# A gather of one slot for 128 tokens, products in four 64x64 tiles, and six kept weight blocks

## The chip, the cores and the metric

The kernel runs on one core of a Trainium2 chip. The metric is the time of one execution on the device in microseconds (us). Before the change it is 1643.7 us, the median of 3 runs (1643.1 to 1644.28 us).

## The reference

Two layers over 256 tokens of width 1024. Each layer mixes tokens (two kinds of attention), then replaces the feed-forward part by an expert retrieval, and closes with a gated addition and a LayerNorm. The change is about the retrieval and what follows it:

```python
for i in range(DEPTH):                                   # 2 layers
    mix = token_mixers(h, w_in[i], w_out[i], ...)        # differential attention + sparse attention
    h = layer_norm(DEEPNORM_ALPHA * h + mix, ln1_g[i], ln1_b[i])
    r = DEEPNORM_ALPHA * h + peer_ffn(h, ...)
    gate = sigmoid(r @ ple_wg[i] + ple_bg[i])
    h = layer_norm(r + gate * (p[i] @ ple_wp[i]), ln2_g[i], ln2_b[i])

def peer_ffn(...):                                       # per token: 8 heads x 16 experts of 16384
    q = xt @ w_q;  s = q . sub_keys                      # 2 x 128 scores a head, top 16 of each half
    best, pos = top_k(all 256 sums, 16); g = softmax(best)
    u, v = u_tab[eidx], v_tab[eidx]                      # 128 rows of u and of v for each token
    return sum_k g_k * gelu(u_k . x) * v_k
```

Each token needs 128 rows of `u` and `v`. They lie side by side in one table (8 KB a pair), so 256 tokens x 128 slots x 2 layers x 8 KB = 537 MB are read.

## The kernel before, in words

The work is four runs (layer x tile of 128 tokens). Run n has a mixing stage (`MIX[n]`: projections, attention, output projection, LayerNorm, choice of the experts) and a closing stage (`CLOSE[n]`: gate, addition, LayerNorm). Four gather phases, one for each run, lie end to end. While phase n fetches and uses the expert rows of run n, the closing of run n-1 and the mixing of run n+1 are done beside it.

A phase has 64 pairs of gathers (`PAIRS`). One gather (L535, issued by GpSimd) brings 128 rows of 8 KB into one of 8 buffers of the ring `rows`. For each pair VectorE takes two dot products with the tokens (L1070) and, every second pair, spreads the softmax weights over small diagonal matrices `idg` (L1062). ScalarE takes the GELU (L707) and scales the diagonals to `dg` (L711). TensorE multiplies `dg` by the v half of the buffer and adds it to the accumulator `acc` in PSUM (L1390, in the last phase L1386). When that is done, GpSimd may refill the two buffers (`pair_done`).

A gather before the change holds four slots of 32 tokens: partition 32a+t is slot 4q+a of token 32c+t. So the index table must be rearranged by small products (`perm`, L1283, copied to `rows_of` and `g_of` in L944 and L945), and the tokens must be spread too: `hx[c]` holds the 32 tokens of block c four times (products L1361, copied by ScalarE through `spread_out`). The product's stationary matrix is 128x32, so a gather's two products fill the 32 partitions of block c.

The order on each engine is written out by hand: the tables (`PROJECT_PLAN`, `ATTEND_PLAN`, `TURN_PLAN`, `CLOSE_PLAN`, `LAST_EARLY`, `LAST_CLOSE`) give a part's pair on PE, ACT and DVE, and `walk` issues the parts of a pair ahead of the pair's own work. The start, before the first pair, is `START_PE`, `START_ACT`, `START_DVE`. Every engine works its list in order.

Weights come in blocks of 1 MB (two units), issued by SyncE in the order in which TensorE uses them (L493), into a ring of four buffers (`WRING`). `KEPT_BLOCKS` (four) have buffers of their own and are loaded once per layer instead of once per run. `EXTRA` (four) are blocks of the first run that land in ring buffers 4 to 7 of `rows` before the gathers need them.

The last phase works in blocks of 32 tokens (order 0, 2, 1, 3): each block is closed as soon as its products are done. Its parts are `ztake` (ScalarE copies it out of `acc`), `zrT` (transposes), `zgate` (bias and gate products L1324, L1332, sigmoid), `zblend` (VectorE L966 to L970), `zsum` (L1340) and `znorm` (L975 to L987). `warm` (L1346) are products whose result nobody reads.

## Time and profile before

| | |
|---|---|
| median of 3 runs | 1643.7 us (1643.1 to 1644.28) |
| profiled execution, its own time | 1645.81 us |
| its span, first to last instruction | 1644.0 us |
| PE, DVE, ACT, POOL busy | 75%, 65%, 29%, 36% of the span |
| moved by the DMA engines | 662.10 MB, 403 GB/s on average |
| mean granted TensorE clock | 0.836 |

PE is TensorE, DVE VectorE, ACT ScalarE, POOL GpSimd, SP SyncE. The busy shares are averages over the whole span. Which resource sets the pace has to be read stretch by stretch. DMA shares can read 1.01 or 1.02 where all 16 DMA engines are busy throughout. A matrix product in 32-bit floats stands as two MATMUL records in the profile.

### The profile page before, as it was taken

How to read it: one execution, taken by the hardware profiler on the slowest of the kernel's cores; microseconds unless marked ns; L12 is line 12 of the kernel's file. 1: busy time of each engine (PE TensorE's matmuls, PEld its weight loads, DVE VectorE, ACT ScalarE, POOL GpSimd, SP SyncE). 2: the span in 40 equal slices, each digit the busy share in tenths (PEclk: the TensorE clock that was granted, in tenths of full speed). 3: DMA queues.
4: the chain of work that ended last, by engine and by line, in shares of the span. 5: the costliest groups of instructions: out<-in, count | busy, mean ns of one | idle time of the engine just before them, and what ended most of it. 6: DMA issues, size and time to landing. Idle time of an engine off the chain costs nothing.

```text
span 1644.0 us, 19823 instructions
## 1 busy us (share of the span) xinstructions
PE 1227.3 (75%) x7210; PEld 620.1 (38%) x7210; DVE 1070.7 (65%) x2773; ACT 479.5 (29%) x1278; POOL 585.3 (36%) x516
## 2 busy tenths in 40 slices
PE   8988958696778789586677969869687767434556
PEld 8655714241452266131442328424253223111223
DVE  1458788755689764654579785584588958655553
ACT  1323224342223423241132422342222323211223
POOL 0013243343334333343334332244344434444441
PEclk9999978897899889897888979979798876555558
DMA  8789999999999999999999999999999999999994
GB/s 315 255 328 412 418 420 410 422 422 421 421 409 406 406 422 420 422 420 422 420 421 421 418 410 412 421 421 422 421 419 417 414 421 414 422 421 421 419 419 166
DMA packets 92625, 662.10 MB, mean 403 GB/s; under 512 B 10288, under 2 KB 11504, under 8 KB 12528
## 3 DMA queue, kind: packets, MB, share of 16 engines
q0 software_dynamic: 73728, 536.90, 78.9%
q1 hardware_dynamic: 18576, 123.81, 18.6%
q8 instruction: 57, 0.93, 0.2%
q14 instruction: 40, 0.33, 0.0%
q10 hardware_dynamic: 224, 0.13, 0.0%
HBM read 659.75 MB, written 1.05 MB: 402 GB/s over the span
## 4 chain that ended last, share of the span: by engine, by line
DMA 38%; PE 30%; DVE 21%; ACT 5%; issue 3%; POOL 3%; ACTq 0%; SPq 0%; DVEq 0%; POOLq 0%
DMA rows<-uv_dram,rows_of 37%; DVE rows L1070 10%; PE bank L1110 9%; PE acc L1390 8%; PE bank L1128 5%; POOL rows L535 3%; PE acc L1386 2%; ACT dg L711 2%; PE bank L1332 1%; ACT ex L630 1%; PE bank L1353 1%; ACT gel L707 1%; DVE i L778 1%; DVE i L769 1%; DVE ex L772 1%
## 5 line engine op out<-in xcount | busy, mean ns | idle before, releaser
L535 POOL DMA_INDIRECT rows<-uv_dram,rows_of x512 | 585.1, 1143 | 1025.4 <-PE acc L1390 663.0
L1070 DVE CUSTOM_DVE_ANT_0 rows<-rows,hx 128x1024 f32<-128x1024 f32 x512 | 618.7, 1224 | 425.8 <-DMA rows<-uv_dram,rows_of 412.7
L1390 PE MATMUL acc<-rows,dg 128*32 128x512 f32 x1536 | 439.7, 707 | 234.6 <-ACT dg L711 232.9
L707 ACT ACTIVATE gel<-dots 128x2 f32<-128x2 f32 x256 | 52.0, 203 | 853.2 <-DVE dots L1070 841.4
L1390 PEld LDWEIGHTS acc<-rows,dg 128*32 128x32 f32 x1536 | 83.5, 119 | 497.5 <-ACT dg L711 323.4
L1110 PEld LDWEIGHTS bank<-xT,wring 128*128 128x128 f32 x1728 | 206.1, 200 | 32.2 <-issue 25.2
L1386 PE MATMUL acc<-rows,dg 128*32 128x256 f32 x1024 | 109.9, 571 | 144.6 <-ACT dg L711 144.6
L1110 PE MATMUL bank<-xT,wring 128*128 128x128 f32 x1728 | 213.0, 285 | 4.4 <-ACT xT L550 2.4
L1128 PE MATMUL bank<-wring,xT 128*128 128x512 f32 x352 | 165.5, 617 | 0.8 <-ACT xT L550 0.7
L711 ACT ACTIVATE dg<-idg,gel 128x32 f32<-128x32 f32 x512 | 137.1, 314 | 23.8
L1386 PEld LDWEIGHTS acc<-rows,dg 128*32 128x32 f32 x1024 | 35.4, 145 | 213.0 <-ACT dg L711 183.8
L1128 PEld LDWEIGHTS bank<-wring,xT 128*128 128x128 f32 x352 | 66.6, 197 | 91.3 <-issue 89.3
L707 ACT ACT_TABLE_LOAD x52 | 66.7, 1283 | 1.2
L1110 PEld LDWEIGHTS bank<-xT,kept 128*128 128x128 f32 x384 | 45.6, 198 | 5.6 <-issue 5.4
L1110 PE MATMUL bank<-xT,kept 128*128 128x128 f32 x384 | 47.6, 284 | 0.0
L550 ACT ACTIVATE probsT<-bank 128x512 f32<-128x512 f32 (+1 forms) x59 | 31.2, 545 | 53.9 <-PE bank L1110 27.2
L1070 DVE DVE_READ_ACCUMULATOR2_ANT dots<- 128x1 f32 x512 | 42.2, 82 | 0.0
L1237 PE MATMUL bank<-prm,fixed 64*128 64x256 f32 x96 | 31.0, 476 | 11.0 <-DVE mixed L957 11.0
L1062 DVE TENSOR_TENSOR idg<-fixed,g_of 128x128 f32<-128x128 f32 x128 | 36.9, 288 | 2.0 <-ACT dg L711 0.5
L1361 PE MATMUL bank<-h,fixed 128*128 128x512 f32 x64 | 31.4, 616 | 0.0
L1237 PEld LDWEIGHTS bank<-prm,fixed 64*128 64x128 f32 x96 | 21.3, 233 | 21.2 <-DVE mixed L957 12.0
L818 DVE SCALAR_TENSOR_TENSOR sc<-fixed,bank 128x128 f32<-128x128 f32 (+1 forms) x32 | 9.1, 349 | 26.7 <-PE bank L1188 26.7
(185 smaller groups left out, 1057.4 us busy)
## 6 DMA issues: line engine op xcount, KB each, us to landing
wring<-wmix_dram SPq DMA_DIRECT2D x84, 1024.0 KB
wring<-wclose_dram SPq DMA_DIRECT2D x15, 1024.0 KB
kept<-wmix_dram SPq DMA_DIRECT2D x8, 1024.0 KB, 18.4
rows<-uv_dram,rows_of POOLq DMA_INDIRECT x512
rows<-wmix_dram SPq DMA_DIRECT2D x4, 1024.0 KB, 12.7
rows<-prm_dram SPq DMA_DIRECT2D x2, 1024.0 KB, 7.9
wring<-wmix_dram SPq DMA_DIRECT2D x4, 512.0 KB
fixed<-fixed_dram SPq DMA_DIRECT2D x1, 576.0 KB, 10.6
```

Source lines behind the costliest of these rows:

```text
L535: pool.indirect_dma_start(out=rows[:, slot, :], out_offset=None, in_=uv_d[phase // TILES], in_offset=bass.IndirectOffsetOnAxis(ap=rows_of[ ...
L550: ins = A(out, src, func)
L707: A(gel[:, s:s + 2], dots[:, s:s + 2], ACT.Gelu).then_inc(gelu_done, 1)
L711: A(dg[:, s + j, :], idg[:, P // 2 % 2, 2 * (P % 2) + j, :], ACT.Identity, scale=gel[:, s + j:s + j + 1]).then_inc(dg_ready, 1)
L1062: V.tensor_tensor(idg[:, P // 2 % 2], ident32[:, None, :].broadcast_to([128, 4, BT]), gates[:, :, None].broadcast_to([128, 4, BT]), ALU.mu ...
L1070: V.tensor_tensor_reduce(out=rows[:, s, 0:D], in0=rows[:, s, 0:D], in1=hx[:, c, :], scale=1.0, scalar=0.0, op0=ALU.mult, op1=ALU.add, accu ...
L1110: ins = MM(bk[:, T * at:T * at + T], w[:, T * c:T * c + T], src[:, c, :], start=(c == 0), stop=(c == KC - 1))
L1128: ins = MM(bk[:], xT[:, 2 * q + c, :], w[:, 512 * c:512 * c + 512], start=(q == 0 and c == 0 and extra is None), stop=(q == 3 and c == 1), ...
L1237: ins = MM(bk[:, QCOLS * j:QCOLS * j + QCOLS], chooser(first + i // 2, 2 * (i % 2) + j), prm[:], start=True, stop=True)
L1361: MM(bk[:], fixed[:, F_SPREAD + 128 * c:F_SPREAD + 128 * c + 128], h[:, 512 * i:512 * i + 512], start=True, stop=True).then_inc(full, 1)
L1386: ins = MM(quarters(acc, c)[BT * k:BT * k + BT, :], dg[:, s, :], rows[:, s, D + 256 * k:D + 256 * k + 256], start=False, stop=False, skip_ ...
L1390: ins = MM(acc[BT * c:BT * c + BT, 512 * i:512 * i + 512], dg[:, s, :], rows[:, s, D + 512 * i:D + 512 * i + 512], start=False, stop=False ...
```

## The change

It has five parts.

1. In the first three phases a gather brings one slot of all 128 tokens (`columns_of`). Its indices are a column of the index table as VectorE computes it, so the `perm` products and copies go in those phases, and the dots read the tokens themselves (`hb`, one buffer for each tile) instead of `hx`. The last phase keeps the old form.
2. The product of a gather in those phases is four products of 64x64 tiles: row half r of the gather, column half j of the output. `dg` is 128x64. The accumulator then holds token half r in PSUM bank r and feature half j in partition half j. So the closing reads `rT` in another order, and new products `nat` bring the rows back to their natural layout.
3. `hx` for the last phase lies in two kept weight blocks, and its spreading matrices in a third, loaded when that block is done. The freed memory makes six kept blocks. Two blocks instead of four are extra.
4. At a turn of phases ScalarE only copies the accumulator (`take`). `mixed` shares the memory of `res`, and the gates that of the queries.
5. In the last phase the third block's closing is laid out anew: gate at pair 59, blend at pair 62 instead of 61, its norm behind the last pair. `warm` is issued twice instead of four times, and the bias products (`zbias`) are a part of their own.

```diff
-def gathers_of(phase, p):
-
-    if phase < RUNS - 1 or p < PAIRS // 2:
-        return [(p // 2, 2 * (p % 2)), (p // 2, 2 * (p % 2) + 1)]
+TILE_ORDER = ((0, 0), (1, 1), (0, 1), (1, 0))
...
+    if phase < LAST or p < PAIRS // 2:
+        return [2 * p, 2 * p + 1]
...
 ]
-TURN_PLAN = [
-    ("hx0", 61, None, None), ("hx1", 62, None, None), ("hx2", 63, None, None),
-    ("hx3", 64, None, None), ("hx", None, 64, None), ("init", 64, None, None),
+TURN_PLAN = [("take", None, 64, None), ("init", 64, None, None)]
+TURN_LAST = [
+    ("hx0", 60, 61, None), ("hx1", 61, 62, None), ("hx2", 62, 63, None),
+    ("hx3", 63, 64, None), ("take", None, 64, None), ("init", 64, None, None),
...
+    ("g1a", 4, None, None), ("g1b", 5, 6, None), ("nat", 6, None, None), ("gb0", 6, 7, None), ("gb1", 7, 8, None),
...
-def last_close(c, at, step=1):
-
-    return [(f"ztake{c}", None, at + 1 * step, None), (f"zrT{c}", at + 2 * step, at + 3 * step, None),
-            (f"zgate{c}", at + 4 * step, at + 5 * step, None), (f"zblend{c}", None, None, at + 5 * step),
-            (f"zsum{c}", at + 6 * step, None, None), (f"znorm{c}", None, at + 7 * step, at + 7 * step)]
-
-
-LAST_EARLY = [("zple", 5, 6, None), ("zgb", 26, 27, None), ("warm0", 60, None, None), ("warm1", 61, None, None),
-              ("warm2", 62, None, None), ("warm3", 63, None, None)]
-for _i in range(BLOCKS - 1):
+def last_close(c, at):
+
+    return [(f"ztake{c}", None, at + 1, None), (f"zrT{c}", at + 2, at + 3, None),
+            (f"zbias{c}", at + 4, None, None), (f"zgate{c}", at + 4, at + 5, None), (f"zblend{c}", None, None, at + 5),
+            (f"zsum{c}", at + 6, None, None), (f"znorm{c}", None, at + 7, at + 7)]
+
+
+LAST_EARLY = [("zple", 5, 6, None), ("zgb", 26, 27, None), ("warm0", 61, None, None)]
+for _i in range(BLOCKS - 2):
     LAST_EARLY += last_close(LAST_ORDER[_i], PAIRS // 2 + PAIRS // 2 // BLOCKS * (_i + 1))
-LAST_CLOSE = last_close(LAST_ORDER[BLOCKS - 1], 0, 0)
+_c, _d = LAST_ORDER[BLOCKS - 2:]
+LAST_EARLY += [(f"ztake{_c}", None, 57, None), (f"zrT{_c}", 58, 59, None), (f"zbias{_c}", 59, None, None), (f"zgate{_c}", 59, 61, None),
+               (f"zblend{_c}", None, None, 62), (f"zsum{_c}", 62, None, None), ("warm1", 62, None, None)]
+LAST_CLOSE = [(f"ztake{_d}", None, 0, None), (f"zbias{_d}", 0, None, None), (f"zrT{_d}", 0, 0, None), (f"znorm{_c}", None, 0, 0),
+              (f"zgate{_d}", 0, 0, None), (f"zblend{_d}", None, None, 0), (f"zsum{_d}", 0, None, None), (f"znorm{_d}", None, 0, 0)]
...
 START_PE = ("wake T par idx dq0 dq1 dk0 dk1 iw ds0 ix sq0 sq1 dv0 dv1 dpt sk0 dpv sk1 ss0 sv0 sv1 mT0 mix0a spt0 spt1 mix1p spv mix1a mT1 "
-            "mix0b mix1b fill h1T pq0a ps0 pq1a init hx0 ps1 hx1 perm0 pq2a hx2 hx3").split()
+            "mix0b mix1b fill h1T pq0a ps0 pq1a init ps1 pq2a").split()
 START_ACT = ("embed0 T par idx dq1 dk1 iw ix exps0 exps1 sq1 dv1 dpt dpv sk1 rms sexp0 sexp1 sv1 mT0 spt0 spt1 mT1 embed1 n1a "
-             "h1T pq0a ps0 C0a pq1a hx0 ps1 hx1 hx2 hx3").split()
-START_DVE = ("embed0 ds0 ix sel0 sel1 wts0 wts1 sel2 sel3 far rms rms2 ss0 merge embed1 n1a n1b A0a B0a C0a C0b perm0").split()
+             "h1T pq0a ps0 C0a pq1a ps1").split()
+START_DVE = ("embed0 ds0 ix sel0 sel1 wts0 wts1 sel2 sel3 far rms rms2 ss0 merge embed1 n1a n1b A0a B0a C0a C0b").split()
...
+            if part[:4] == "perm" and run.n < LAST:
+                continue
...
-EXTRA_SLOT = 4
-EXTRA = [tuple(units_of(part)) for part in ("pq1a", "pq2a", "pq2b", "pq3a")]
+EXTRA_SLOT = 6
+EXTRA = [tuple(units_of(part)) for part in ("pq1a", "pq2a")]
 
 KEPT = WRING + len(EXTRA)
-KEPT_BLOCKS = [(U_SK, U_SK + 1)] + [tuple(units_of(part)) for part in ("pq3b", "pq4a", "pq4b")]
+KEPT_BLOCKS = [tuple(units_of(part)) for part in ("pq2b", "pq3a", "pq3b")] + [(U_SK, U_SK + 1)] + [
+    tuple(units_of(part)) for part in ("pq4a", "pq4b")]
+HX_BLOCKS, SPREAD_BLOCK = 2, 2
...
-        hx = sb("hx", [128, BLOCKS, D])
+        hx = kept[:, 0:HX_BLOCKS, :].rearrange("p b (a d) -> p (b a) d", d=D)
+        spread = kept[:, SPREAD_BLOCK, 0:128 * BLOCKS]
-        h, res, mixed = (sb(n, [128, D]) for n in ("h", "res", "mixed"))
+        hb, res = sb("hb", [128, TILES, D]), sb("res", [128, D])
+        mixed = res
...
+                if part == "hx0":
+                    sp.wait_ge(*block_done[KEPT + SPREAD_BLOCK, run.layer])
+                    sp.dma_start(spread, fixed_d[:, FCOLS:FCOLS + 128 * BLOCKS]).then_inc(spread_landed, 16)
...
-                        if EXTRA_SLOT <= k < RING:
+                        if EXTRA_SLOT <= k < EXTRA_SLOT + len(EXTRA):
                             pool.wait_ge(*block_done[WRING + k - EXTRA_SLOT, 0])
                         pool.indirect_dma_start(
                             out=rows[:, slot, :], out_offset=None, in_=uv_d[phase // TILES],
...
-                            in_offset=bass.IndirectOffsetOnAxis(ap=rows_of[:, phase % 2, 4 * q + c:4 * q + c + 1], axis=0),
+                            in_offset=bass.IndirectOffsetOnAxis(ap=rows_of[:, phase % 2, col:col + 1], axis=0),
...
-                    for i in range(2):
-                        take(run, f"rT{i}", quarter(xT, i))
+                    for r in range(2):
+                        act.wait_ge(*full_at(run, f"rT{r}"))
+                        bk, taken = bank_of(run, f"rT{r}")
+                        A(xT[:, :, HT * r:HT * r + HT].rearrange("p (j k) t -> p j k t", j=2),
+                          bk[:].rearrange("p (k j t) -> p j k t", k=4, j=2), ACT.Copy).then_inc(taken, 1)
...
-                if part == "hx":
-                    if n:
-                        act.wait_ge(dot_ready, 4 * QUADS * n)
-                    for c in range(BLOCKS):
-                        if n and c == 2:
-                            taking(CLOSE[n - 1])
-                        spread_out(run, c)
+                if part == "take":
+                    taking(CLOSE[n - 1])
...
-                    A(dg[:, s + j, :], idg[:, P // 2 % 2, 2 * (P % 2) + j, :], ACT.Identity, scale=gel[:, s + j:s + j + 1]
+                    w = HT if phase < LAST else BT
+                    A(dg[:, s + j, 0:w], idg[:, P // 2 % 2, 2 * (P % 2) + j, 0:w], ACT.Identity, scale=gel[:, s + j:s + j + 1]
...
+                    bk, taken = bank_of(run, f"nat{i}")
+                    for name in banks_of(run, "nat"):
+                        dve.wait_ge(*full_at(run, name))
+                    V.tensor_tensor(half_of(res, i), bk[:], half_of(gates, i), ALU.add).then_inc(taken, 1)
+                    dve.wait_ge(*taken_at(run, f"nat{i}"))
...
-                        dve.wait_ge(out_stored, 16)
...
+                    if n < LAST:
+                        V.scalar_tensor_tensor(rows_of[:, n % 2, at], sel[:, 0, 0:gs], float(NKEYS), sel[:, 1, 0:gs], ALU.mult, ALU.add
+                                               ).then_inc(rows_picked, 1)
...
+                    w, one = (HT, ident64) if phase < LAST else (BT, ident32)
+                    V.tensor_tensor(idg[:, P // 2 % 2, :, 0:w], one[:, None, :].broadcast_to([128, 4, w]),
+                                    shares[:, :, None].broadcast_to([128, 4, w]), ALU.mult).then_inc(idg_ready, 1)
...
+                    if phase < LAST:
+                        if col == 0:
+                            dve.wait_ge(h1_ready, 2 * phase + 2)
+                        tokens = hb[:, phase % TILES, :]
+                    else:
+                        if col < BLOCKS:
+                            dve.wait_ge(hx_ready, col + 1)
+                        tokens = hx[:, col % BLOCKS, :]
...
+                if part == "nat":
+                    for j in range(2):
+                        bk, full = bank(run, f"nat{j}")
+                        at = slice(HT * j, HT * j + HT)
+                        for r in range(2):
+                            ins = MM(bk[HT * r:HT * r + HT, :], ident[at, at], res[at, 512 * r:512 * r + 512], start=True, stop=True,
+                                     skip_group_check=True)
+                        ins.then_inc(full, 1)
...
+                    pe.wait_ge(h1_ready, 2 * n + 2)
+                    for r, j in TILE_ORDER:
+                        at = slice(HT * r, HT * r + HT)
+                        MM(acc[HT * j:HT * j + HT, 512 * r:512 * r + 512], ident_a[at, at], h_of(run)[at, 512 * j:512 * j + 512],
+                           start=True, stop=False, skip_group_check=True)
...
-                        ins = MM(acc[BT * c:BT * c + BT, 512 * i:512 * i + 512], dg[:, s, :],
-                                 rows[:, s, D + 512 * i:D + 512 * i + 512], start=False, stop=False, skip_group_check=True)
+                    for r, j in TILE_ORDER:
+                        at = slice(HT * r, HT * r + HT)
+                        ins = MM(acc[HT * j:HT * j + HT, 512 * r:512 * r + 512], dg[at, s, :], rows[at, s, D + 512 * j:D + 512 * j + 512],
+                                 start=False, stop=False, skip_group_check=True)
```

On SyncE's queue these are the weight loads of the second run's mixing and what follows, before and after the change (`wring` is the weight ring, `wmix` the mixing weights, `wclose` the closing weights). Before:

```order
L493 DMA wring<-wmix_dram 128x2048 x9
L493 DMA kept<-wmix_dram 128x2048
L493 DMA rows<-wmix_dram 128x2048 x4
L493 DMA kept<-wmix_dram 128x2048 x3
L493 DMA wring<-wmix_dram 128x2048
L493 DMA wring<-wmix_dram 128x1024
L493 DMA wring<-wmix_dram 128x2048 x21
L493 DMA wring<-wclose_dram 128x2048
```

After:

```order
L515 DMA wring<-wmix_dram 128x2048 x9
L515 DMA kept<-wmix_dram 128x2048
L515 DMA rows<-wmix_dram 128x2048 x2
L515 DMA kept<-wmix_dram 128x2048 x5
L515 DMA wring<-wmix_dram 128x2048
L515 DMA wring<-wmix_dram 128x1024
L515 DMA wring<-wmix_dram 128x2048 x19
L515 DMA wring<-wclose_dram 128x2048
```

The first run's two blocks moved from `rows` to `kept`, and the second run issues 19 whole blocks instead of 21. The fourth run's list changes in the same way.

On PE at the start, from the transposes of h to the first pair's product (L1100 or L1138 are transposes, L1110 or L1148 query products, L1273 or L1311 key products, L1374 or L1424 the accumulator's start). Before:

```order
L1100 MATMUL bank<-fixed,h 128x128 x8
L1110 MATMUL bank<-xT,wring 128x128 x16
L1273 MATMUL bank<-kept,probsT 128x128 x2
L1110 MATMUL bank<-xT,rows 128x128 x16
L1374 MATMUL acc<-h,fixed 128x512 x2
L1361 MATMUL bank<-h,fixed 128x512 x2
L1273 MATMUL bank<-kept,probsT 128x128 x2
L1361 MATMUL bank<-h,fixed 128x512 x2
L1283 MATMUL bank<-chosen,fixed 32x8 x16
L1110 MATMUL bank<-xT,rows 128x128 x16
L1361 MATMUL bank<-h,fixed 128x512 x4
L1110 MATMUL bank<-xT,rows 128x128 x16
```

After:

```order
L1138 MATMUL bank<-fixed,hb 128x128 x8
L1148 MATMUL bank<-xT,wring 128x128 x16
L1311 MATMUL bank<-kept,probsT 128x128 x2
L1148 MATMUL bank<-xT,rows 128x128 x16
L1424 MATMUL acc<-hb,fixed 64x512 x4
L1311 MATMUL bank<-kept,probsT 128x128 x2
L1148 MATMUL bank<-xT,rows 128x128 x16
L1148 MATMUL bank<-xT,kept 128x128 x16
L1442 MATMUL acc<-rows,dg 64x512 x8
```

The spreading products and the index products are gone, and the accumulator's start is four 64-wide products.

On DVE at the end, the third block's blend and norm (L966 to L970 and L975 to L987; after the change L987 to L991 and L996 to L1007) among the dots of the last pairs. Before:

```order
L970 BN_STATS stats<-res 128x6
L1070 ISA rows,dots<-rows,hx 128x1024
L1070 ISA dots 128x1
L1070 ISA rows,dots<-rows,hx 128x1024
L1070 ISA dots 128x1
L1062 TENSOR_TENSOR idg<-fixed,g_of 128x128
L1070 ISA rows,dots<-rows,hx 128x1024
L1070 ISA dots 128x1
L1070 ISA rows,dots<-rows,hx 128x1024
L1070 ISA dots 128x1
L975 BN_AGGR mv<-bank 128x2
```

After:

```order
L991 BN_STATS stats<-res 128x6
L1094 TENSOR_TENSOR idg<-fixed,g_of 128x4x32
L1108 ISA rows,dots<-rows,kept 128x1024
L1108 ISA dots 128x1
L1108 ISA rows,dots<-rows,kept 128x1024
L1108 ISA dots 128x1
L1108 ISA rows,dots<-rows,kept 128x1024
L1108 ISA dots 128x1
L1108 ISA rows,dots<-rows,kept 128x1024
L1108 ISA dots 128x1
L996 BN_AGGR mv<-bank 128x2
```

Before, the blend lies ahead of the dots of pair 61 and the norm ahead of those of the last pair, 63. After, the blend lies ahead of pair 62 and the norm behind all dots.

## Rows read from the trace of the kernel before

**Rows 1.** The page: DMA engines' busy tenths in 40 slices, and GB/s.

```profile
DMA  8789999999999999999999999999999999999994
GB/s 315 255 328 412 418 420 410 422 422 421 421 409 406 406 422 420 422 420 422 420 421 421 418 410 412 421 421 422 421 419 417 414 421 414 422 421 421 419 419 166
```

**Rows 2.** Busy time of each engine in stretches, with granted clock, DMA share and GB/s.

```profile
core 0: us, PE busy (x) PEld busy (x) DVE busy (x) ACT busy (x) POOL busy (x), PEclk, DMA share, GB/s
111.00:119.00 8.00, 6.88 (x64) 4.25 (x63) 6.88 (x30) 3.04 (x7) 1.31 (x2) 1.00 0.02 7
135.00:488.00 353.00, 275.67 (x1604) 146.10 (x1605) 254.46 (x694) 103.95 (x284) 130.72 (x118) 0.87 1.01 418
488.00:524.00 36.00, 27.63 (x128) 9.34 (x129) 34.62 (x107) 14.08 (x34) 15.55 (x14) 1.00 0.97 389
524.00:960.00 436.00, 337.11 (x1688) 157.73 (x1685) 284.63 (x732) 130.72 (x344) 161.23 (x140) 0.89 1.01 419
960.00:1000.00 40.00, 30.52 (x147) 15.03 (x146) 37.95 (x107) 12.61 (x34) 17.71 (x14) 0.79 0.99 399
1618.00:1623.00 5.00, 2.75 (x20) 1.01 (x19) 4.42 (x9) 1.20 (x6) 0.00 (x0) 0.87 0.13 54
```

**Rows 3.** Waits: engine line <- released by: us in total, times, longest.

```profile
POOL rows L535 <- PE acc L1390: 663.0, 181, 10.6
DVE rows L1070 <- DMA rows<-uv_dram,rows_of: 412.7, 257, 3.8
```

**Rows 4.** Timeline, PE's products in a middle stretch: start us, us, instructions.

```profile
628.13 1.71 PE L1188 MATMUL bank<-dkT,dqT 64*128 64x128 f32 x16
629.77 1.92 PE L1390 MATMUL acc<-rows,dg 128*32 128x512 f32 x8
631.62 0.72 PE L1196 MATMUL bank<-ikT,iqT 64*128 64x128 f32 x8
```

**Rows 5.** Groups of instructions by form: busy us, mean ns, idle before.

```profile
L1361 PE MATMUL bank<-h,fixed 128*128 128x512 f32 x64 | 31.4, 616 | 0.0
L1062 DVE TENSOR_TENSOR idg<-fixed,g_of 128x128 f32<-128x128 f32 x128 | 36.9, 288 | 2.0 <-ACT dg L711 0.5
L1022 DVE TENSOR_TENSOR ex<-posf,fixed 128x256 f32<-128x256 f32 x16 | 6.8, 422 | 0.3
```

**Rows 6.** Timeline, start: from the chosen indices to the first gather's issue.

```profile
115.70 0.17 DVE L1043 SCALAR_TENSOR_TENSOR chosen<-sel 128x16 f32<-128x16 f32 x1
116.93 0.18 DVE L944 CAST rows_of<-bank 128x16 uint32<-128x16 f32 x1 [0.57 <-PE bank L1283]
117.39 1.07 POOL L535 DMA_INDIRECT rows<-uv_dram,rows_of  x1 [116.94 <-DVE rows_of L944]
```

**Rows 7.** Timeline, the third block's closing and the last pairs.

```profile
1608.87 1.23 DVE L1070 CUSTOM_DVE_ANT_0 rows<-rows,hx 128x1024 f32<-128x1024 f32 x1 [1.25 <-DMA rows<-uv_dram,rows_of]
1616.30 0.43 DVE L966 TENSOR_TENSOR mixed<-mixed,val 128x256 f32<-128x256 f32 x1 [6.20 <-ACT mixed L550]
1621.89 3.59 PE L1346 MATMUL bank<-fixed 128*128 128x512 f32 x4
1626.30 0.27 DVE L975 BATCH_NORM_AGGREGATE mv<-bank 128x2 f32<-128x24 f32 x1 [3.89 <-PE bank L1340]
1628.92 1.22 DVE L1070 CUSTOM_DVE_ANT_0 rows<-rows,hx 128x1024 f32<-128x1024 f32 x1
1631.07 0.59 PEld L1386 LDWEIGHTS acc<-rows,dg 128*32 128x32 f32 x16 [2.71 <-ACT dg L711]
1631.07 1.07 PE L1386 MATMUL acc<-rows,dg 128*32 128x256 f32 x16 [1.89 <-ACT dg L711]
```

**Rows 8.** Timeline: one block's gate products twice, and the same pair product.

```profile
1567.91 4.93 PE L1332 MATMUL bank<-wring,xT 128*32 128x256 f32 x64
1586.41 1.94 PE L1386 MATMUL acc<-rows,dg 128*32 128x256 f32 x16 [2.94 <-ACT dg L711]
1633.57 3.66 PE L1332 MATMUL bank<-wring,xT 128*32 128x256 f32 x64
```

159 lines of the change are left out of this document (82 added, 77 removed), and 3 rows, old and new, of tables (CLOSE_LAST, CLOSE_PLAN).

## The prediction

> **What bounds the kernel now.** I read the DMA lines of the page first. From the fourth of 40 slices to the last but one the DMA engines are 90% busy or more and move 406 to 422 GB/s. Only the first 120 us and the last slice are lower [rows 1]. The table of stretches says the same more sharply: DMA share 1.01 and 418 to 419 GB/s in the long stretches, while PE is busy for 275.7 of 353 us (78%) [rows 2]. So for nine tenths of the span the bytes set the time. Then the waits: GpSimd waits 663 us for PE's products to free ring buffers, and VectorE 412.7 us for rows to land [rows 3]. That is a full ring behind a saturated DMA, not a slow PE. What is left for the rest is what happens before the first gather, two shallow dips at turns of phases, and the tail behind the last rows.
>
> **Part 1, six kept blocks: 9.9 us.** Runs 2 and 4 each issue two whole weight blocks fewer, which the queue's rows in the section on the change show. The first run loads the same blocks into other buffers. Four blocks of 1.049 MB at 419 GB/s [rows 2] are 4 x 2.50 = 10.0 us. The spreading matrices and the shorter constants add 32 KB net, 0.1 us. Both phases in which the loads fall are saturated, so the 9.9 us come off the span if PE can walk 1.3% faster there. It has 22% idle time. Bounds: 0 (something else paces these phases at once) and 10.
>
> **Part 2, the start: 1.2 us.** The index column is ready in 115.70, 0.17 us long. Before the change it went through PE and was copied only at 116.93, and the gather was issued at 117.39, 0.28 us after that copy's end [rows 6]. Now the instruction of 115.70 writes `rows_of` itself: 115.70 + 0.17 + 0.28 = 116.15, 1.24 us earlier. The DMA engines stand still meanwhile (share 0.02 from 111 to 119 [rows 2]), so this counts in full. The eight spreading products of the start go too (31.4 us for 32 such products, 0.98 each [rows 5], 7.9 us on PE), but VectorE's choice is what the gather waits for, so I give nothing for it. Bounds: 0 and 1.5.
>
> **Part 3, the turns: 1 us.** Before, the first dots of a phase had to wait until ScalarE had copied all of `hx`, which could only start behind the old phase's last dots. Now they need only h and their rows. At the two turns with a dip the DMA share is 0.97 for 36 us and 0.99 for 40 us, against 1.01 [rows 2]: 1.4 + 0.8 = 2.2 us lost. The accumulator must still be copied and restarted ahead of the first product, so I take 1.0. Bounds: 0 and 2.2.
>
> **Part 4, the products of 64x64 tiles: nothing.** Today a pair is 4 products, 8 records, 1.92 us at full clock [rows 4]. Only two column blocks are in it, so two records run at a time: four steps of 0.43 us and 0.2 us around them. Each new product fills a quarter of the array as the old one did, but a pair has 8 of them, 16 records. Four at a time gives four steps again, 1.92 us. Two at a time gives 8 x 0.43 + 0.2 = 3.6 us, one at a time 7.1 us. The trace has four column tiles at once: the last phase's pair is 16 records of half the width in 1.07 us, 0.2 us around four steps of 0.216 us [rows 7]. It has two row tiles at once: 8 records of L1196 take 0.72 us, where 16 of L1188, issued in longer groups for each row half, take 1.71, 0.107 each, one after the other [rows 4]. Rows and columns together it does not have. I take 1.92 us, because both nearest rows overlap fully when the tiles alternate as closely as they do here. Up to 3.3 us (below) it costs nothing either way.
>
> A rule of the Trainium skill speaks against this. Its page "TensorE: Matmul & The Clock Gate", section "The mechanism", says that a weight load overlaps products in flight only if its row group is another. Two of our four tiles share a row group with their forerunners. By that rule some loads would be exposed and a pair would be nearer to the 3.6 us. The trace disagrees: the four column tiles of [rows 7] share one row group, and their 16 loads lie within the first 0.59 us of the 1.07. The page "TensorEngine Tiling (Array Packing)", "Gotcha 1", says that different row tiles must not write one PSUM bank at the same time. The new form gives row half r bank r, so the rule costs nothing here, and no row of before shows its price.
>
> **Part 5, VectorE and ScalarE: nothing.** `idg` doubles to 256 columns: 0.29 us becomes 0.42 (a 256-column operation of the same kind) [rows 5], 0.13 x 96 = 13 us over three phases, and the index copies and 24 of 32 `hx` halves' copies go. VectorE is busy for 254 of 353 us and the dots wait for rows [rows 2, 3], which hides it. The new `nat` products (four a closing, three closings) are 12 of at most 0.98 us on PE, whose idle time hides them. If that cover is gone they cost up to 12 us.
>
> **Part 6, the end: 4 us.** Most engines have delivered the last rows by 1618, stragglers until 1623 (share 0.13 [rows 2]). But VectorE is in order and stands idle for 6.2 us until the third block's gate is through ScalarE at 1616.30, and for 3.9 us until its sums are there at 1626.30. The sums were behind idle products (L1346, 3.59 us at 1621.89). So the last dot starts only at 1628.92, and its product at 1631.07 [rows 7]. After the change the gate is one pair earlier, the blend one pair later, and nothing lies before the last dots. The last dot can start when its row is there, about 1623.0. From there on the chain is the old one, so it ends 5.9 us earlier. The norm of the third block slips under the last block's gate products. Something is late next: the clock. The last gate ran at 2.4 GHz in 3.66 us, behind four sets of idle products. Two sets are gone. The same 64 records took 4.93 us where they began at 1.2 GHz and got 2.4 on the way, and the pair product takes 1.94 us at 1.2 GHz instead of 1.07 [rows 8]. That gives back 0 (clock kept) to 4.5 us (all at 1.2 GHz: 3.7 + 0.9). I take 1.9. The end gains 4.0 us, bounds 1.4 and 5.9.
>
> **Sum.** 9.9 + 1.2 + 1.0 + 0 + 0 + 4.0 = 16.1 us. The profiled execution took 1645.8 us, 1.8 us of it outside its span of 1644.0. That makes 1629.7 us. The median of the runs is 2.1 us below the profiled execution, so the forecast is 1627.6 us. With each term at its likely bounds (loads 9 to 10, start 1 to 1.5, turns 0 to 2.2, end 1.4 to 5.9) the gain is 11.4 to 19.6, 1624.1 to 1632.3 us.
>
> **Rivals.**
>
> *A, the tiles run two at a time (slower).* A pair's product is 3.6 us, 1.7 us more. From 135 to 1000 us PE is busy for 671 of 865 us and serves 143 pairs [rows 2], so it has 194 us idle, 1.36 us a pair. From 3.3 us a pair on PE is the bound. At 3.6 it needs 246 us more, 52 more than it has. If half of its idle time can't be used, since products wait for their rows, it is 149. Over 192 pairs that is 70 to 200 us: some 1700 to 1830 us, 1740 near its lower end. For it: no row has rows and columns tiled together. Against it: both halves of the pattern overlap. 5%.
>
> *B, a gather of 128 tokens' same slot moves fewer bytes per us (slower).* The indices of a gather are now the same rank of one head for all tokens, not four ranks of 32. If the rows of one gather fall worse on the memory, the rate drops. In slices 13 and 14 the same gathers ran at 406 GB/s instead of 421 [rows 1], 3.6%. Over 384 gathers of 2.5 us that is 34 us: 1627.6 + 34 = 1662 us. It decides from a rate below 414 on. Against it: every row is 8 KB wherever it lies, and the engines read at a full share throughout. 4%.
>
> *C, the end does not get shorter.* The stragglers of the last gather or the clock take it all: 1627.6 + 4 = 1632 us. 14%.
>
> *D, the loads saved are not given back,* because the pace of the second or fourth run's mixing is set by its own chain of parts: half of part 1 is lost, 1633, or all of it, 1637.5. For it: the parts are tied to pairs, and the waits on PE are long. Against it: the DMA share of 1.01. 10%.
>
> *E, more than I count* (deeper prefetch through kept blocks closes more of the dips, the start gains from a freer PE): 1622 us. 7%.
>
> *F, no effect at all*, because the freed buffers and the shorter queues only move waits: 1643. 4%.
>
> The forecast has the other 56%. Faster by over 0.2% (3.3 us, about what a measurement of this kernel can tell from no change) are the forecast, C, D and E: 87%. F is within it: 4%. A and B are slower: 9%. The range for 8 in 10 takes in E's and D's times: 1620 to 1638 us. It leaves out A, B, F and what lies beyond, some 15%.
>
> **What would show it.** The product's line must have 3072 records in three phases, 16 a pair in about 1.9 us at full clock. At 3.6 us A is right. The bytes must be about 658 MB with a rate of 418 GB/s or more in the long stretches; below 414 B is right. The first gather must be issued near 116.1 us. The stretch between the first gathers of the second and third phase holds no saved load and should shorten by 1 us at most, those of the first and third phase by 5 each. If they don't, D is right. At the end the last dot must wait for its row and for nothing else, and the last gate's 64 records show the clock: 3.7 us, or 5 and more. I am wrong if PE is busy over 95% in the long stretches, or if VectorE waits in the last pairs for anything but rows.

## The result, and the profile after

The changed kernel takes 1638.14 us (median of 13 runs, 1629.99 to 1641.75), the kernel before 1646.61 us beside it (13 runs, 1643.1 to 1653.32). The ratio is 0.9943 [0.9927, 0.9959]: 9.4 us faster. Forecast were 16.1 us and a time of 1627.6 us, with a range of 1620 to 1638.

The page of the changed kernel's profiled execution (its own time 1641.7 us):

```profile
span 1639.9 us, 21801 instructions
DMA  8689999999999999999999999999999999999994
GB/s 314 252 342 398 412 420 384 423 421 421 421 419 372 420 377 421 421 421 421 420 421 421 420 421 415 420 421 414 420 421 420 420 420 409 422 422 421 421 421 183
DMA packets 92201, 658.07 MB, mean 401 GB/s; under 512 B 10240, under 2 KB 11456, under 8 KB 12608
```

658.07 MB were moved instead of 662.10: the four saved blocks of 1.049 MB, less 0.16 MB of other transfers. Yet the mean rate fell. Against [rows 1] the slices from the 25th on are about as good. The new dips are the 4th, 7th, 13th and 15th slice: 398, 384, 372 and 377 GB/s.

The stretches of [rows 2], in the changed kernel:

```profile
core 0: us, PE busy (x) PEld busy (x) DVE busy (x) ACT busy (x) POOL busy (x), PEclk, DMA share, GB/s
135.00:488.00 353.00, 279.38 (x1892) 151.84 (x1884) 258.95 (x684) 107.14 (x284) 135.39 (x117) 0.87 1.00 413
488.00:524.00 36.00, 22.72 (x116) 6.58 (x120) 34.66 (x103) 10.79 (x27) 12.81 (x12) 0.76 0.94 366
524.00:960.00 436.00, 334.63 (x2060) 161.23 (x2052) 284.42 (x715) 130.58 (x335) 159.80 (x140) 0.87 1.01 416
960.00:1000.00 40.00, 28.57 (x182) 12.82 (x183) 37.99 (x105) 11.82 (x35) 15.03 (x13) 0.75 1.01 416
1618.00:1623.00 5.00, 1.34 (x17) 0.42 (x16) 2.96 (x8) 0.81 (x5) 0.00 (x0) 0.86 0.03 13
```

The first turn (488 to 524 us) fell from 389 to 366 GB/s, and TensorE's clock there from 1.00 to 0.76. VectorE is busy for 34.66 of the 36 us, as it was before. The second turn (960 to 1000 us) got better, 399 to 416 GB/s. The last bytes come some 2.5 us earlier.

The products of the new form, in the groups by line and in the timeline (start us, us). These rows answer to [rows 4], [rows 5] and [rows 6]:

```profile
L1442 PE MATMUL acc<-rows,dg 64*64 64x512 f32 x3072 | 463.4, 728 | 248.7 <-ACT dg L735 248.6
L1094 DVE TENSOR_TENSOR idg<-fixed,g_of 128x256 f32<-128x256 f32 (+1 forms) x128 | 49.8, 389 | 2.0
```

```profile
115.34 0.17 DVE L1065 SCALAR_TENSOR_TENSOR rows_of<-sel 128x16 uint32<-128x16 f32 x1
115.80 1.07 POOL L560 DMA_INDIRECT rows<-uv_dram,rows_of  x1 [115.34 <-DVE rows_of L1065]
...
501.70 3.69 PE L1442 MATMUL acc<-rows,dg 64*64 64x512 f32 x16 [1.74 <-ACT dg L735]
506.91 1.95 PE L1442 MATMUL acc<-rows,dg 64*64 64x512 f32 x16 [1.52 <-ACT dg L735]
...
628.21 1.95 PE L1442 MATMUL acc<-rows,dg 64*64 64x512 f32 x16
```

A pair of 16 records takes 1.95 us at 2.4 GHz and 3.69 us at 1.2 GHz. The second figure is no tiling effect: it nearly doubles with the clock.

The end, in the timeline, answering to [rows 7]:

```profile
1616.28 1.23 DVE L1108 CUSTOM_DVE_ANT_0 rows<-rows,kept 128x1024 f32<-128x1024 f32 x1 [1.13 <-DMA rows<-uv_dram,rows_of]
1621.20 1.23 DVE L1108 CUSTOM_DVE_ANT_0 rows<-rows,kept 128x1024 f32<-128x1024 f32 x1 [1.23 <-DMA rows<-uv_dram,rows_of]
...
1616.31 1.96 PE L1386 MATMUL bank<-fixed 128*128 128x512 f32 x4
1618.43 1.07 PE L1437 MATMUL acc<-rows,dg 128*32 128x256 f32 x16 [0.16 <-ACT dg L735]
1623.36 1.94 PE L1437 MATMUL acc<-rows,dg 128*32 128x256 f32 x16 [3.85 <-ACT dg L735]
1625.22 1.08 PE L1361 MATMUL bank<-prm,fixed 64*32 64x256 f32 x8
1626.23 0.69 PE L1356 MATMUL bank<-fixed,res 128*128 128x128 f32 x2
1627.39 5.81 PE L1372 MATMUL bank<-wring,xT 128*32 128x256 f32 x64 [0.47 <-ACT xT L575]
```

The last dots now wait for rows alone. But the clock is at 1.2 GHz from the last pair on: its product takes 1.94 us, and the last gate 5.81 us, against 1.07 and 3.66 in [rows 7, 8].

**An account of the span.** The span splits into three parts that can be read from the DMA records of any profile here: up to the first gather, from it to the last gathered byte, and from there to the end. The middle part is compared with what its bytes need at 422.8 GB/s (on each of 16 engines an 8 KB packet every 310 ns; in these traces 309 ns is the commonest and 312 ns the median time of such a packet). The rest of it is called the lost time: engines dry, or packets slower than that.

| profiled run | first gather | bytes need | lost time | last byte to end | span |
|---|---|---|---|---|---|
| before | 117.4 | 1481.4 | 24.5 | 20.8 | 1644.0 |
| changed | 115.8 | 1472.4 | 32.6 | 19.1 | 1639.9 |

So 9.0 us of bytes are gone, the end is 1.7 us shorter, the start 1.6 us, and 8.1 us came back as lost time. The experiments are read by the same account, because the start of one kernel differs by up to 7 us from execution to execution (110.6 to 117.4 us in the 18 profiles here, in both families), which would drown a term of 1 us. Each line of the account is one execution: the same kernel, profiled twice, lost 32.6 and 30.6 us.

The prediction also named the distances between the first gathers of the phases as a sign. They went from 378.4 to 379.0 us in the first phase, from 399.9 to 403.9 in the second and from 385.3 to 379.3 in the third. Only the third shortened as forecast.

### The profile page after: what moved, and what is told of

The parts are those of the page before. It is cut to its first block, busy times and chain, and to the rows that moved or that the text cites. A ratio compares the mean times of both kernels' runs of the same rounds, so it can differ in the third digit from the quotient of the medians.

```text
span 1639.9 us, 21801 instructions
## 1 busy us (share of the span) xinstructions
PE 1212.4 (74%) x8246; PEld 625.5 (38%) x8246; DVE 1081.0 (66%) x2743; ACT 477.5 (29%) x1257; POOL 589.1 (36%) x516
## 2 busy tenths in 40 slices
DMA packets 92201, 658.07 MB, mean 401 GB/s; under 512 B 10240, under 2 KB 11456, under 8 KB 12608
## 4 chain that ended last, share of the span: by engine, by line
DMA 37%; PE 32%; DVE 19%; ACT 5%; POOL 3%; issue 3%; ACTq 0%; SPq 0%; POOLq 0%; DVEq 0%
DMA rows<-uv_dram,rows_of 37%; PE bank L1148 9%; PE acc L1442 9%; DVE rows L1108 9%; PE bank L1166 6%; POOL rows L560 3%; PE acc L1437 2%; ACT dg L735 2%; PE bank L1372 1%; PE bank L1138 1%; PE bank L1401 1%; ACT ex L655 1%; DVE idg L1094 1%; ACT gel L730 1%; DVE i L802 1%
## 5 line engine op out<-in xcount | busy, mean ns | idle before, releaser
L1108 DVE CUSTOM_DVE_ANT_0 rows<-rows,hb 128x1024 f32<-128x1024 f32 x384 | 463.2, 1223 | 316.6 <-DMA rows<-uv_dram,rows_of 315.3
L1442 PE MATMUL acc<-rows,dg 64*64 64x512 f32 x3072 | 463.4, 728 | 248.7 <-ACT dg L735 248.6
L1442 PEld LDWEIGHTS acc<-rows,dg 64*64 64x64 f32 x3072 | 113.5, 154 | 512.9 <-ACT dg L735 346.2
L1108 DVE CUSTOM_DVE_ANT_0 rows<-rows,kept 128x1024 f32<-128x1024 f32 x128 | 155.5, 1224 | 113.9 <-DMA rows<-uv_dram,rows_of 113.5
L1148 PEld LDWEIGHTS bank<-xT,wring 128*128 128x128 f32 x1536 | 181.8, 199 | 25.9 <-issue 18.8
L1148 PE MATMUL bank<-xT,wring 128*128 128x128 f32 x1536 | 187.6, 284 | 4.7 <-DVE sc L842 2.9
L735 ACT ACTIVATE dg<-idg,gel 128x64 f32<-128x64 f32 (+1 forms) x512 | 147.0, 334 | 24.6 <-ACT gel L730 0.7
L1437 PEld LDWEIGHTS acc<-rows,dg 128*32 128x32 f32 x1024 | 35.3, 146 | 218.6 <-ACT dg L735 190.0
L1148 PEld LDWEIGHTS bank<-xT,kept 128*128 128x128 f32 x640 | 73.7, 193 | 14.1 <-issue 14.1
L1148 PE MATMUL bank<-xT,kept 128*128 128x128 f32 x640 | 77.0, 279 | 0.0
L1094 DVE TENSOR_TENSOR idg<-fixed,g_of 128x256 f32<-128x256 f32 (+1 forms) x128 | 49.8, 389 | 2.0
## 6 DMA issues: line engine op xcount, KB each, us to landing
wring<-wclose_dram SPq DMA_DIRECT2D x15, 1024.0 KB, 10.4
```

The source lines that it names most:

```text
L735: A(dg[:, s + j, 0:w], idg[:, P // 2 % 2, 2 * (P % 2) + j, 0:w], ACT.Identity, scale=gel[:, s + j:s + j + 1]).then_inc(dg_ready, 1)
L1094: V.tensor_tensor(idg[:, P // 2 % 2, :, 0:w], one[:, None, :].broadcast_to([128, 4, w]), shares[:, :, None].broadcast_to([128, 4, w]), ALU ...
L1108: V.tensor_tensor_reduce(out=rows[:, s, 0:D], in0=rows[:, s, 0:D], in1=tokens, scale=1.0, scalar=0.0, op0=ALU.mult, op1=ALU.add, accum_out ...
L1148: ins = MM(bk[:, T * at:T * at + T], w[:, T * c:T * c + T], src[:, c, :], start=(c == 0), stop=(c == KC - 1))
L1437: ins = MM(quarters(acc, c)[BT * k:BT * k + BT, :], dg[:, s, 0:BT], rows[:, s, D + 256 * k:D + 256 * k + 256], start=False, stop=False, sk ...
L1442: ins = MM(acc[HT * j:HT * j + HT, 512 * r:512 * r + 512], dg[at, s, :], rows[at, s, D + 512 * j:D + 512 * j + 512], start=False, stop=Fal ...
```

## The experiments

Each kernel was timed in five rounds beside the kernel before on the same chip. Four kernels at a time shared a chip: a_same, a_heat, a_warm3 and a_reload; a_oldend, b_newend, a_actidg and a_dbl; a_nat, c_warm3, c_heat and a_tiles; a_narrow, a_repair, b_dbl and b_actidg. Ratios are to the kernel before.

**a_same: the changed kernel itself.** It is the base of the others.

> The changed kernel itself once more, as the measure for the runs beside it. Theory (slow products at the turns): again 7 to 10 us below the kernel before, DMA engines dry for 3 to 4 us more than before in the stretches where VectorE is over 90% busy (140 to 180, 260 to 290, 490 to 600 us), and pair products of 3.5 us and more there where the granted clock is at its lower level. Rival (slower gathers as such): the rate is lower also in the long stretches where VectorE has time to spare.

1635.6 us, ratio 0.9931 [0.9913, 0.9948]. Account: first gather 110.8, lost 30.6, last byte to end 18.4, span 1632.1. So the gain is 9 to 11 us by the two measurements.

**a_reload: two of the six kept blocks are loaded again in the second and fourth run.**

```
-    return [b for b in blocks if not (run.stage == "mix" and run.tile and b in KEPT_BLOCKS)]
+    return [b for b in blocks if not (run.stage == "mix" and run.tile and b in KEPT_BLOCKS[HX_BLOCKS:])]
```

> The two blocks kept in addition are loaded again in the second and fourth run, as before the change: 4 x 1.049 MB more. Theory (bytes set the time): 8 to 10 us slower than the changed kernel, so about the time of the kernel before. Rival (the phases that lost loads are paced by their own chain, the saved loads are not given back): at most 5 us slower.

1645.97 us, ratio 0.999 [0.9978, 1.0002]: 10.4 us above a_same. Its weights' queue moved 4.2 MB more:

```profile
q1 hardware_dynamic: 18720, 123.84, 18.5%
```

With the bytes of before, and all else changed, the time of before is nearly back. Lost time is 31.5 us, as in the changed kernel. The saved loads give what they should. Everything else in the change together gives 1 to 2 us (by the interval between nothing and 3.6), where 6.2 were forecast. The distances between first gathers say the same of each phase: 383.3 and 384.2 us in the first and third, 377.1 and 378.5 in a_same.

**a_heat: idle products at the first two turns,** four sets of two in each, to hold the clock.

```
+TURN_PLAN = [("heat0", 61, None, None), ("heat1", 62, ...), ("heat2", 63, ...), ("heat3", 64, ...), ("take", ...
```

> Four sets of two 128x512 products that nobody reads stand where the spreading products of the first two turns stood. Theory (the removed products had kept the clock at 2.4 GHz over the turn, and slow pair products let the DMA engines run dry): granted clock about 1.0 from 490 to 530 us, first pair product of the second phase 1.95 instead of 3.6 us, DMA share there back to 0.98, and the kernel 1.5 to 4 us faster than the changed kernel. Rival (VectorE alone sets the pace at the turn): clock up, time the same within 1 us or up to 2 us slower, since the products stand in the way of the pairs.

1636.14 us, ratio 0.993 [0.9912, 0.9948], the same as a_same. The turn itself did change:

```profile
488.00:524.00 36.00, 30.13 (x151) 10.64 (x150) 34.69 (x103) 10.95 (x28) 15.21 (x13) 1.00 0.97 391
```

Clock 1.00 and 391 GB/s, as before the change. Lost time is 29.1 us, 1.5 less than in a_same, and the last byte to end is 19.9, 1.5 more. The time shows no gain, but the interval would let 4 us of either sign pass, and the idle products themselves stand in the way of the pairs. So this run does not price the clock at the turn.

**a_warm3: a third warm set at pair 63.**

```
+               ..., ("warm1", 62, None, None), ("warm2", 63, None, None)]
```

> One more set of idle products ahead of the last pair's product. Theory (the end lost 3 to 4 us to the lower clock): last pair product 1.1 instead of 1.9 us, last gate 3.7 instead of 5.8 us, 2 to 3.5 us faster than the changed kernel. Rival (the chain from the last landed row sets the end in any case): no more than 0.5 us, or slower if the set delays the last product.

1634.59 us, ratio 0.9915 [0.9901, 0.9929], about 1 us below a_same, which its interval does not separate. In the timeline of its end:

```profile
1621.88 1.07 PE L1437 MATMUL acc<-rows,dg 128*32 128x256 f32 x16 [1.94 <-ACT dg L735]
...
1624.37 3.66 PE L1372 MATMUL bank<-wring,xT 128*32 128x256 f32 x64 [0.47 <-ACT xT L575]
```

The clock holds, and the last byte to end is 15.4 us. Three other kernels (a_tiles, a_narrow, a_actidg) have 15.4 to 15.5 us without this set. So two sets hold the clock in some executions, in three of the ten profiles that have two. Three or four sets held it in all eight.

**a_oldend and b_newend: the order of the end alone,** taken back in the changed kernel, and put into the kernel before.

```
-LAST_EARLY += [(f"ztake{_c}", None, 57, None), (f"zrT{_c}", 58, 59, None), (f"zbias{_c}", 59, None, None), ...
-LAST_CLOSE = [(f"ztake{_d}", None, 0, None), (f"zbias{_d}", 0, None, None), (f"zrT{_d}", 0, 0, None), ...
+LAST_CLOSE = last_close(LAST_ORDER[BLOCKS - 1], 0, 0)        # a_oldend; b_newend the other way round
```

> The changed kernel with the order of the end as it was before: the third quarter's bias, gate and sum and the fourth's take come after the last pair again, the bias stands behind the transposes, four warm sets at pairs 60 to 63. What is computed is the same. If the end is worth what the forecast gave it (4.0 us), this run lies 4.0 us above the changed kernel (1635.6 us in the calls before), at 1639 to 1640. If the end is worth little, because TensorE stands at 1.2 GHz behind the last pair of the changed kernel (last gate 5.81 us there against 3.66 before, last dot to the end of the span 18.7 against 15.1 us) and one warm set more brought only 1 us, it lies 0 to 1.5 us above, at 1635.5 to 1637.

> The kernel before with the changed kernel's order of the end and nothing else of the change. Full value of the end: 4.0 us below the kernel before. Little value: 0 to 1.5 us below it. If it is 4 here and less than 1.5 in the changed kernel, the end is worth its price only where the last gathers land as in the kernel before.

a_oldend: 1638.7 us, ratio 0.9939 [0.9917, 0.9961]. b_newend: 1642.36 us, ratio 0.9977 [0.9961, 0.9992], so 3.8 us faster than before, between 1.3 and 6.4. a_oldend's interval allows no difference and 4 us. The last byte to end is 20.8 us in before and 18.2 in b_newend, 19.3 in a_oldend against 19.1 and 18.4 in the changed kernel. Over all profiles it is 20.3 to 20.8 us in the three with the old end in the kernel before, and 15.4 to 19.9, 18.1 on average, in the nine variants of the changed kernel with the new end and two warm sets. The end's new order is worth 0.4 to 5.4 us from execution to execution, and 2.4 on average. In a_oldend VectorE waits 3.88 us for sums ahead of the last pair's dots, as in [rows 7], but the clock is kept (last dot to end 15.0 us). In b_newend the wait is gone and the clock too:

```profile
1620.91 1.94 PE L1393 MATMUL acc<-rows,dg 128*32 128x256 f32 x16 [3.85 <-ACT dg L716]
...
1624.94 4.79 PE L1339 MATMUL bank<-wring,xT 128*32 128x256 f32 x64 [0.47 <-ACT xT L555]
```

With the third warm set both are had: 15.4 us, 5.4 less than before.

**a_actidg: the diagonals are built by ScalarE.**

```
-   V.tensor_tensor(idg[:, P // 2 % 2, :, 0:w], one[...], shares[...], ALU.mult).then_inc(idg_ready, 1)      # VectorE, every second pair
+   A(idg[:, P // 2 % 2, 2 * (P % 2) + j, 0:w], one, ACT.Identity, scale=g_of[:, phase % 2, col:col + 1])     # ScalarE, ahead of the pair's GELU
```

> The changed kernel with the gated diagonals (idg) built by ScalarE, two of 128x64 a pair, where VectorE built four at a time in 0.42 us every second pair; what is computed is the same. VectorE loses 0.21 us a pair, in all 96 x 0.42 + 32 x 0.29 = 50 us of busy time; ScalarE (27% busy) gains about 0.33 us per token column. Theory V: the DMA engines go dry at the turns and at 570 to 600 us because VectorE is over 90% busy there and a pair costs it 5.8 us where the gathers need 5.05; each of some 30 such pairs then gives back 0.21 us: 5 to 8 us, 1628 to 1631. Theory N: VectorE's load is not what makes the ring dry (the slow clock of TensorE or the order of the loads is): within 1.5 us of the changed kernel, or slower by what the fuller ScalarE costs.

1630.95 us, ratio 0.9905 [0.9886, 0.9924]: 4.3 us below a_same by the ratios, at the edge of the noise. The groups by line show where the work went:

```profile
L741 ACT ACTIVATE idg<-fixed,g_of 128x64 f32<-128x64 f32 (+1 forms) x512 | 143.5, 329 | 3.2 <-DVE g_of L1089 1.7
```

The new instructions take 143.5 us on ScalarE, and those that went had 49.8 on VectorE. On the pages ScalarE's busy time rises from 477.5 to 596.3 us and VectorE's falls from 1081.0 to 1041.6. Lost time falls to 26.2 us. Two more pairs of kernels below differ in the diagonals alone: by the ratios c_warm3 is 4.0 us below a_warm3, and c_heat 5.3 us below a_repair, with 25.8 against 31.6 and 25.0 against 31.3 us lost. Three times the same: this gain is shown.

**a_dbl: each diagonal is built twice by VectorE.**

```
+   V.tensor_tensor(idg[:, P // 2 % 2, :, 0:w], ...).then_inc(L.sem, L.one()); settle()      # and then the same again
```

> The changed kernel with each gated diagonal built twice in the same place by VectorE (0.42 us more every second pair, 0.29 in the last phase, and a wait for its own result). Theory V: the mirror of the run that takes it away, 5 to 8 us slower (1641 to 1644); by the same slope the widening from 0.29 to 0.42 us in the change itself cost some 1.5 to 2.5 us. Theory N: within 1.5 us of the changed kernel, and the widening cost nothing.

1639.07 us, ratio 0.9947 [0.9926, 0.9968]: 2.6 us above a_same, where 5 to 8 were expected. The intervals overlap, and the changed kernel's other measurement was 0.9943, so the time shows no difference. Lost time is 35.9 us, 5 more than in a_same and 3 more than in the first profile of the changed kernel.

**b_actidg and b_dbl: the same two edits in the kernel before,** where a diagonal is 32 wide (37 us less, 37 us more).

> The kernel before with the gated diagonals built by ScalarE: VectorE loses 37 us. Same sensitivity as in the changed kernel: 2 to 3.5 us faster than the kernel before (ratio 0.998 to 0.9985). If the kernel before had slack on VectorE, under 1 us either way, and the changed kernel is the one in which the load on VectorE counts.

> The kernel before with each gated diagonal built twice in its place: VectorE gets 128 x 0.29 = 37 us more, and a wait for its own result. If the kernel before is as sensitive as the changed one (0.05 to 0.09 us for each us of VectorE's load): 2 to 3.5 us slower than the kernel before. If it had slack: under 1 us.

b_actidg: 1645.16 us, ratio 0.9994 [0.9975, 1.0013], lost time 25.2 us. b_dbl: 1648.92 us, ratio 1.0007 [0.9992, 1.0023], lost time 28.9 us. The kernel before shows nothing to gain from a lighter VectorE (25.2 against 24.5 and, in b_newend, 26.3 us lost). With a heavier one its one profile lost some 4 us more, but its time did not move beyond its interval. That the kernel before stands at a knee over which the change pushed it is therefore not shown.

**a_narrow: diagonals 32 wide in the changed kernel,** with the other columns set to zero once at the start. Half of each product is left out of the result.

```
-                    w, one = (HT, ident64) if phase < LAST else (BT, ident32)
+                    w, one = BT, ident32
```

> The changed kernel with the gated diagonals written 32 wide, as before the change; the other 32 columns are zero, so half of each product is left out of the result, while products, their shapes and gathers are unchanged. Only VectorE's load falls, by 96 x 0.13 us = 12.5 us. If the time goes with VectorE's load along the whole way (50 us less gave 4.3 us of time, 49 us more cost 2.6): 0.6 to 1.1 us below the changed kernel (1635), and dry or slow time of the gather stretch 30. If the widening is what ate the missing time: 4 to 5 us below (1631), dry or slow time 25 to 26 us as before the change.

1634.18 us, ratio 0.9916 [0.99, 0.9933], lost time 30.0 us. The time is 1 to 2.5 us below a_same, which the intervals do not separate, and the lost time is that of the changed kernel. VectorE is busy for 1068.5 us on this page, where the kernel before has 1070.7 and loses 24.5. So more load on VectorE as a whole is not what loses the time.

**a_nat: the `nat` products a pair earlier.**

```
-    ("g1a", 4, None, None), ("g1b", 5, 6, None), ("nat", 6, None, None), ...
+    ("g1a", 4, None, None), ("nat", 5, None, None), ("g1b", 5, 6, None), ...
```

> The changed kernel with the products that turn the layer's result back to natural order (nat) issued one pair earlier in the closing, ahead of the second half of the gate's products; what is computed is the same. In the changed kernel VectorE waits 2.8 us for them at 547 us, with the dots of the next pair queued behind, some 10 us before the stretch in which it is over 90% busy and the DMA engines go dry. If that wait is what starts the dry stretch of 565 to 600 us (11.1 us dry or slow in the second phase, 4.5 before), the wait is gone, that figure falls by 2 to 3 us and the time by as much, to 1633. If the slack of 560 us is refilled anyway, the wait goes and the time stays (1635.6).

1634.96 us, ratio 0.9926 [0.99, 0.9953], lost time 31.5 us. VectorE's wait for them (2.80 us at 550 us in the changed kernel) is gone. The time stays within its interval.

**a_repair: third warm set, `nat` earlier and the idle products at the first turn,** with VectorE's load left alone.

> The changed kernel with the third warm set, nat a pair earlier and the idle products at the first turn alone, but with the diagonals left to VectorE. If clock and wait are worth something only together: 3 to 4 us below the changed kernel (1632) and dry or slow time of 27 to 28 us. If only VectorE's load counts in the gather stretch: 1 to 2 us below (1634), all of it from the warm set at the end (last dot to end 15.0 us), and dry or slow time 30 to 32 us.

1636.11 us, ratio 0.9914 [0.9892, 0.9936], lost time 31.3 us, last byte to end 15.4 us. All that it gains by the account is at the end. But its idle products, a pair later than those of a_heat, did not hold the clock:

```profile
488.00:524.00 36.00, 28.35 (x124) 9.22 (x128) 34.66 (x105) 10.23 (x27) 12.94 (x11) 0.81 0.93 367
```

Clock 0.81 and 367 GB/s, where a_heat had 1.00 and 391. So it does not tell what clock and wait are worth together.

**a_tiles: the four tiles of a token in another order,** neighbours on the same rows.

```
-TILE_ORDER = ((0, 0), (1, 1), (0, 1), (1, 0))
+TILE_ORDER = ((0, 0), (0, 1), (1, 0), (1, 1))
```

> The changed kernel with the four 64x64 tiles of a token in the order row 0 column 0, row 0 column 1, row 1 column 0, row 1 column 1, where neighbours now share their rows; what is computed is the same. If two tiles on the same rows overlap like the others, a pair stays at 1.95 us at the full clock and the time at 1635.6. If neighbours on the same rows wait for each other, a pair takes up to 3.6 us, PE's busy time grows by up to 300 us and the kernel is slower by what isn't hidden: 2 us at each turn, 6 us or more.

1635.68 us, ratio 0.9928 [0.9902, 0.9954]. A pair takes the same:

```profile
629.12 1.95 PE L1442 MATMUL acc<-rows,dg 64*64 64x512 f32 x16
629.11 0.21 PEld L1442 LDWEIGHTS acc<-rows,dg 64*64 64x64 f32 x8
```

**c_warm3 and c_heat: repairs put together.** c_warm3 is a_actidg with the third warm set. c_heat has also `nat` earlier and the idle products at the first turn.

> The changed kernel with the diagonals built by ScalarE (1630.95 us by itself) and a third warm set at pair 63. The warm set holds the clock for the last gate: last dot to end 15.0 us, where the changed kernel has 17.9 to 18.7. If this holds in each run and not only in the one profiled: 1 to 3 us below the run with the diagonals alone, 1628 to 1630. If the run with the diagonals alone had it already (its profiled run has 15.0 us): no difference, 1631.

> All repairs in one kernel: diagonals by ScalarE, third warm set, nat a pair earlier, and four sets of two idle 128x512 products at pairs 62 to 65 of the first turn alone. If clock, the wait for nat and VectorE's load together are the cause of the second phase's dry time, it falls from 11.1 to about 5 us (4.5 in the kernel before), the stretch of gathers to 1495 us, and the time to 1625 to 1627, which is what the forecast for the change was. If the clock is no cause (the idle products alone moved nothing before), it stays within 1 us of the kernel without them, at 1628 to 1631.

c_warm3: 1630.49 us, ratio 0.9891 [0.9865, 0.9917], lost time 25.8 us. c_heat: 1626.81 us, ratio 0.9882 [0.9857, 0.9907], lost time 25.0 us, last byte to end 15.6. Both beat the kernel before and the changed kernel, and the two are not told apart by their intervals. In c_heat's second phase 7.7 us are lost, not the 5 expected. c_heat did reach the forecast time, by repairs that the change did not contain.

**Where the time is lost.** The windows of the first 64 gathers of the first phase and of the second phase (first gather to 64th), for before, changed, a_dbl and c_heat in this order, the columns as in [rows 2]:

```profile
117.39:310.10 192.71, 154.04 (x973) 88.91 (x973) 150.84 (x433) 54.94 (x148) 69.88 (x64) 0.87 1.00 411
495.78:703.31 207.53, 166.21 (x863) 81.18 (x861) 144.43 (x391) 71.77 (x187) 77.12 (x65) 0.91 1.01 416
```

```profile
115.80:313.16 197.36, 152.13 (x1064) 89.26 (x1063) 152.81 (x428) 53.04 (x143) 75.19 (x64) 0.86 0.99 402
494.80:707.44 212.64, 168.38 (x1020) 82.56 (x1020) 145.43 (x384) 70.84 (x182) 71.64 (x65) 0.85 0.99 403
```

```profile
115.66:312.53 196.87, 151.79 (x1064) 89.59 (x1064) 158.49 (x441) 52.68 (x142) 72.85 (x64) 0.88 0.99 403
494.85:707.89 213.04, 168.33 (x1020) 82.99 (x1020) 151.05 (x397) 69.21 (x180) 70.40 (x64) 0.86 0.98 398
```

```profile
113.97:308.13 194.16, 146.88 (x1054) 86.18 (x1053) 147.17 (x413) 68.72 (x204) 72.43 (x64) 0.90 1.00 411
489.19:699.90 210.71, 173.04 (x1036) 85.45 (x1036) 140.00 (x367) 85.83 (x245) 77.03 (x64) 0.88 1.00 409
```

The changed kernel takes 4.7 and 5.1 us longer for these two stretches. By the DMA records, the first 32 gathers behind the first turn hold 3.0 to 3.2 us of lost time in before, b_newend and b_actidg, and 5.1 in b_dbl. They hold 5.5 to 9.0 in the ten profiles of the changed kernel and its variants in which VectorE builds each diagonal once, 11.4 in a_dbl, and 3.8 to 6.9 in the three with ScalarE's diagonals. The first 32 gathers of all hold 4.1 to 5.0 before (7.2 in b_dbl), 5.5 to 7.6 in those ten, and 4.9 to 5.7 with ScalarE's diagonals. Behind the second turn it is 1.0 us after against 2.2 before.

The window of the 32 gathers behind the first turn, for before, changed, a_narrow, a_heat and a_tiles in this order:

```profile
495.78:591.32 95.54, 74.80 (x297) 26.52 (x296) 85.15 (x234) 36.50 (x84) 40.29 (x33) 0.87 1.00 409
494.80:594.09 99.29, 74.75 (x363) 26.58 (x364) 85.95 (x232) 35.28 (x79) 37.54 (x33) 0.79 0.97 386
491.50:591.34 99.84, 73.57 (x363) 25.92 (x364) 84.49 (x231) 34.92 (x79) 36.32 (x32) 0.78 0.96 385
488.21:583.86 95.65, 73.33 (x373) 26.06 (x372) 84.50 (x229) 34.24 (x78) 39.79 (x33) 0.89 0.99 398
487.94:585.18 97.24, 72.82 (x363) 26.43 (x364) 85.84 (x230) 34.84 (x79) 40.67 (x33) 0.78 0.99 397
```

VectorE is busy for 84.5 to 86 us of it in all five. a_narrow loses 8.9 us here, as much as the changed kernel (8.6), so no cost of the widening shows here. TensorE's granted clock is what differs: 0.87 to 0.89 in the four profiles of the kernel before and its variants, 0.77 to 0.86 in all variants of the changed kernel but the two in which idle products held it, a_heat and c_heat (0.89). a_heat loses 5.5 us, the least of its ten. But a_tiles loses 5.8 at 0.78, and c_warm3 3.8 at 0.80 against 5.3 in c_heat. The clock may be part of the cause, and these runs do not show it.

## Why the prediction was wrong

In short: the step that failed is the cover that I assumed for the stretch of gathers. I let Part 3 give 1.0 us back at the turns and priced Part 5 at nothing, because "the dots wait for rows [rows 2, 3], which hides it". The runs show lost time in that stretch rising from 24.5 to 32.6 us in the two profiles, and from 25.3 to 31.1 on average over three profiles before and nine after. Besides, Part 6 was sized at 4.0 us and measured 2.4 on average. What exactly in the change lost the time in the stretch stays open.

**Part 1, the loads, 9.9 us: right.** The stretch of gathers needs 9.0 us less at the full rate, and loading two blocks again in two runs costs 10.4 us. Rival D, that the saved loads are not given back, is false as a mechanism of the loads: they shorten the first phase by 6.3 us and the third by 5.7 (a_reload against a_same). By the sign that I had named, D would be right for the first phase, which did not shorten against the kernel before. The sign could not tell a load that is not given back from time that is lost anew.

**Part 2, the start, 1.2 us: right in itself, and lost at once.** The gather follows the choice by 0.46 us (115.34 to 115.80), where 1.69 us lay between before [rows 6], 1.2 us less. But the first 32 gathers then lose 1 to 2 us more. The window of 140 to 170 us, in before and after:

```profile
140.00:170.00 30.00, 24.77 (x184) 15.13 (x184) 27.87 (x86) 7.05 (x23) 11.74 (x11) 0.94 1.00 403
140.00:170.00 30.00, 24.67 (x194) 14.70 (x195) 28.40 (x85) 7.50 (x22) 11.68 (x10) 0.94 0.97 378
```

VectorE is busy for 28.40 of 30 us, and was for 27.87 before. That rows which arrive earlier only wait for their dots, with the ring full, fits these lines, and b_dbl's 7.2 us in its first 32 gathers fit it too. It is argued: no run took the start back alone.

**Part 3, the turns, 1.0 us: wrong.** I read the lost time at the two turns as a wait for the copies of `hx` and gave half of it back. The second turn did gain 1.2 us. The first lost 5.6 us more in the 32 gathers behind it, and 2 to 6 in the other profiles. In [rows 2] VectorE is busy for 34.62 of 36 us there, and 37.95 of 40 us at the second. I used only the DMA share of these rows. It counts a slow packet as work: by their GB/s, 389 and 399 against 419, some 4.5 us were lost in the two windows, not 2.2. The new kernel has the same busy time of VectorE at both turns and lost more at one and less at the other, so that busy time alone does not decide either.

**Part 5, VectorE and ScalarE, nothing: the step that failed, with Part 3.** I said that "VectorE is busy for 254 of 353 us and the dots wait for rows [rows 2, 3], which hides it". That is a mean over stretches. In some VectorE is over 90% busy: 140 to 170 us, the first turn, and 560 to 600 us, here in before and after:

```profile
560.00:600.00 40.00, 30.77 (x135) 13.79 (x134) 37.97 (x96) 13.77 (x35) 15.45 (x13) 0.74 1.00 407
560.00:600.00 40.00, 26.28 (x156) 12.10 (x156) 37.20 (x93) 12.75 (x33) 14.77 (x12) 0.70 0.98 376
```

That the cover is not whole is shown: the diagonals taken off VectorE, 50 us of its instructions, give 4.0 to 5.3 us of time in three pairs of kernels, and 4.4 to 6.3 us of lost time. What the widening itself costs is not shown. It is 12.5 us of load, so by that slope an estimate is 1 us, and a_narrow's time agrees within its noise. Nor is a busy VectorE by itself the loss: it was busier in the lines above before the change, at 407 GB/s and not 376, and a_same has 363 GB/s there with VectorE busy for 34.09 us. I had named 12 us as the cost without that cover, and left it out of the range.

**Part 4, the 64x64 tiles, nothing: right.** 1.95 us for 16 records, where 8 records of the old form took 1.92 [rows 4]. Rival A (3.6 us a pair) is false. It is false with neighbours on the same rows too. The rule of the Trainium skill that I weighed (page "TensorE: Matmul & The Clock Gate", section "The mechanism": a weight load overlaps only products of another row group) does not hold for these small tiles. In a_tiles 8 of a pair's 16 loads are done within 0.21 us, while the first four records of products, each 0.64 us long in the trace, run on both row groups. The section also lets a load into the background weight buffer go ahead, and the trace does not tell which loads those are.

**Part 6, the end, 4.0 us: right in mechanism, too large.** The last dots wait for rows alone, as forecast. The last byte to end is 1.7 us shorter in the two profiles and 2.4 on average. The clock took more than the 1.9 us I gave it: last dot to end 18.7 us instead of 15.1, 3.6 us. That lies within the bounds of 0 to 4.5. The dots themselves gave 5.2 us of the 5.9 forecast: the last one starts 0.5 us behind the last byte (1620.7 us) instead of 5.7. 5.2 less 3.6 is 1.6. In the other variants of the changed kernel with two warm sets it is 0.9 to 2.4 where the clock fell and 5.3 to 5.4 where it held. Rival C, that the end does not get shorter, was half true.

**The sum.** In before, b_newend and b_actidg 24.5 to 26.3 us are lost, in nine profiles with the changed kernel's load on VectorE 29.0 to 32.9. So by the profiles the change is 9.0 us of bytes, 2.4 us on average at the end and 0 to 1.2 at the start, less about 6 us of lost time and nothing for the tiles: 5 to 7 us. The timed runs say 9 to 11. Some 4 us between the two are not accounted for. Profiled executions are few, and those of b_newend and b_actidg took 4 us less than their kernels' medians. The forecast gave Parts 2, 3 and 5 no negative value in its range, so it missed a time 0.14 us above it.

**What stays open.** The cause of the 2 to 6 us that the changed kernel loses more behind the first turn, and of the 1 to 2 us at the start. VectorE's busy time hardly changes in the 64 gathers behind the first turn (144.43 to 145.43), and the widening is not it (a_narrow loses 8.9 us there). Without the wait for `nat` 6.9 us are lost there (a_nat), with the clock held at the turn 5.5 (a_heat), against 8.6 and 8.9 in the changed kernel. Each is one profile, a_tiles has 5.8 with neither, and no time moved beyond its interval. No run had both with the clock really held and VectorE's diagonals left alone. ScalarE's diagonals make up for the whole in time, but they show that VectorE's load counts, not that the change lost its time there. That the order of the new gathers (one slot of 128 tokens) is slower on the memory is not it: from the 25th slice to the end of the third phase they run at 414 to 421 GB/s.

## What to carry to other kernels

Where the DMA engines bound a kernel by nine tenths, their share and an engine's mean busy time over hundreds of us do not say that an addition is hidden. Look at each dip, and by GB/s: a share of 0.97 hid 7% of the rate here. Before an edit is priced at nothing, take the load away and add it in a run each. Taking it away paid here in three pairs of kernels, and in the kernel before it showed nothing. Test the widened part by itself too, since the engine whose load matters need not be where the change lost its time. And split the span at the first gather and the last byte, over many profiles: a term of 2 us at the end varied by 4.5 us with the clock from execution to execution.

## What the runs showed of the hardware

- 32-bit products of 64x64 tiles run four at a time in either order of the tiles: 16 records in 1.95 us at 2.4 GHz, 3.69 us at 1.2 GHz.
- An idle product of TensorE can be worth its time at the end of a kernel: with two warm sets ahead of the last pairs the clock was kept in three of ten profiles, with three or four sets in all eight. From the last dot to the end it is worth some 3 to 4 us in this kernel (14.9 to 15.1 us where the clock was kept, 17.8 to 19.4 where it was not).
- Without the spreading products TensorE's granted clock at the first turn fell from 1.00 to 0.76 (0.86 in a_same), and idle products in their place gave 1.00 again (a_heat). In the profile with 0.76 a pair's products let GpSimd go on only some 4 us behind their start (501.7 to 505.7 us) instead of 2.2 us (498.2 to 500.4 us in the kernel before).
- ScalarE builds a 128x64 diagonal in 336 ns. VectorE makes four in 423 ns, yet the kernel is faster with ScalarE doing it: 143.5 us of instructions on the idler engine for 50 on the busier one.
- The first gather of one and the same kernel was issued at 115.8 us in one profiled execution and at 110.8 us in another.
